# The third expert's second set in one stationary operand: 64 high and 64 low columns

## What is computed

```python
logits = (xt @ router).astype(jnp.float32)
top_logit, top_idx = lax.top_k(logits, TOP_K)          # 2 of 8
gates = jax.nn.softmax(top_logit, axis=-1)
...
yb = _swiglu(xb, w1[e], w3[e], w2[e])                  # silu(x @ w1) * (x @ w3) @ w2, inner width 1408
...
out = jax.ops.segment_sum(y_s * weight_s[:, None].astype(y_s.dtype), token_s, num_segments=T)
```

## Time and profile before

| | us |
|---|---|
| median of 3 runs | 1962.29 |
| lowest, highest | 1961.26, 1963.87 |
| the profiled execution | 1962.09 |
| its span, first to last instruction | 1960.3 |

### The profile page before, as it was taken

One profiled execution on the slowest core, in us unless ns is written; L12 is line 12 of the kernel. 1 busy time (PEld: TensorE's weight loads), 2 busy tenths in 40 slices (PEclk: granted clock), 3 DMA queues, 4 the chain that ended last, 5 costly groups with the idle time before them and its releaser, 6 DMA issues.

```text
span 1960.3 us, 34244 instructions
## 1 busy us (share of the span) xinstructions
PE 1901.8 (97%) x14547; PEld 1749.6 (89%) x14547; DVE 1307.3 (67%) x1851; ACT 941.6 (48%) x1144; POOL 124.2 (6%) x82
## 2 busy tenths in 40 slices
PE   9999999999999999999999999999999999889999
PEld 9889999999988999988788888888888989779988
DVE  7974567645699547666454557888889456866563
ACT  5353344443444433444344346767657443444364
POOL 0000000000000000000101010011200001100034
PEclk9999999999999999999999999999999999999999
DMA  7221345555532123445445467999965323315320
GB/s 306 87 87 57 109 170 204 172 187 179 180 127 87 71 87 135 168 188 174 164 154 180 153 223 276 332 329 333 330 213 184 116 100 124 125 44 173 127 89 23
DMA packets 52679, 321.84 MB, mean 164 GB/s; under 512 B 6320, under 2 KB 9648, under 8 KB 19760
## 3 DMA queue, kind: packets, MB, share of 16 engines
q1 hardware_dynamic: 52096, 317.76, 46.2%
q10 hardware_dynamic: 432, 1.90, 0.3%
HBM read 317.01 MB, written 1.05 MB: 162 GB/s over the span
## 4 chain that ended last, share of the span: by engine, by line
PE 77%; DVE 15%; ACT 4%; issue 3%; DMA 0%; DVEq 0%; ACTq 0%; SPq 0%
PE b L383 76%; DVE s_arena L399 6%; DVE s_ring_lo L501 4%; ACT s_wh L408 2%; PE b L2044 1%; DVE s_arena L402 1%; DVE s_arena L1433 1%; DVE s_arena L2396 1%; ACT s_arena L408 0%; ACT s_arena L405 0%; DVE s_arena L637 0%; DMA s_ring<-experts 0%; DVE s_arena L2320 0%; DVE s_roots L399 0%; DVE s_arena L2317 0%
## 5 line engine op out<-in xcount | busy, mean ns | idle before, releaser
L501 DVE TENSOR_TENSOR s_ring_lo<-s_ring,s_wh 128x2048 fp32r<-128x2048 f32 (+3 forms) x310 | 648.0, 2095 | 315.0 <-ACT s_wh L408 313.9
L408 ACT ACTIVATE s_wh<-s_ring 128x2048 fp32r<-128x2048 f32 (+3 forms) x332 | 574.1, 1732 | 262.8 <-PE b L383 257.1
L383 PE MATMUL b<-s_Hh,s_wh 128*128 128x256 f32 x1832 | 535.3, 292 | 10.0 <-DVE s_arena_r L2923 4.5
L383 PE MATMUL b<-s_Hl,s_wh 128*128 128x256 f32 x1832 | 520.7, 284 | 0.0
L383 PE MATMUL b<-s_Hh,s_ring_lo 128*128 128x256 f32 x1832 | 520.4, 284 | 0.0
L383 PEld LDWEIGHTS b<-s_Hh,s_wh 128*128 128x128 f32 x1832 | 353.5, 193 | 20.9 <-issue 11.0
L383 PEld LDWEIGHTS b<-s_Hl,s_wh 128*128 128x128 f32 x1832 | 353.9, 193 | 0.5
L383 PEld LDWEIGHTS b<-s_Hh,s_ring_lo 128*128 128x128 f32 x1832 | 353.5, 193 | 0.0
L383 PE MATMUL b<-s_wh,s_arena_r 128*128 128x512 f32 (+1 forms) x964 | 305.2, 388 | 3.2 <-DVE s_arena_r L2235 2.6
L383 PE MATMUL b<-s_arena_r,s_wh 128*128 128x256 f32 x1184 | 214.5, 282 | 5.3 <-DVE s_arena L399 2.8
L383 PEld LDWEIGHTS b<-s_wh,s_arena_r 128*128 128x128 f32 x964 | 180.0, 188 | 41.8 <-DVE s_arena_r L2235 3.9
(11 more groups left out here) (193 smaller groups left out, 1962.0 us busy)
## 6 DMA issues: line engine op xcount, KB each, us to landing
s_ring<-fixed SPq DMA_DIRECT2D x158, 1024.0 KB, 4.8
s_ring<-experts SPq DMA_DIRECT2D x96, 1024.0 KB, 5.0
s_ring<-experts SPq DMA_DIRECT2D x48, 768.0 KB, 4.4
s_ring<-fixed SPq DMA_DIRECT2D x24, 256.0 KB, 4.2
s_c<-c SPq DMA_DIRECT2D x1, 1664.0 KB, 17.8
s_ring<-fixed SPq DMA_DIRECT2D x3, 512.0 KB, 6.0
s_arena<-s_arena SPq DMA_DIRECT2D x48, 32.0 KB, 1.9
s_c<-c ACTq DMA_DIRECT2D x1, 1344.0 KB, 6.5
```

Of the source, the lines that this page charges most:

```text
L383: return e.matmul(out, l, r, start=start, stop=True, skip_group_check=True)
L408: return e.activation(out, x, ACT.Copy, scale=scale)
L501: e.tensor_tensor(l_, r_, h_.bitcast(F), SUB).then_inc(*up(engine, z % "lo", i))
```

## The change

The routing now ranks all experts by their count of tokens (key: 8 x count - index), in place of only parting those over 128 from the others. The third turn's second set, (p, s) = (2, 1), is taken to hold 64 slots at most. Its stationary operand of 128 columns holds the high parts of 64 tokens in columns 0..63 and their low parts in 64..127, in `m_H` and likewise in `m_hid`. Two matmuls, with the high and with the low weights, stand where `mm3` had three. The sums of the high parts then stand in rows 0..63 of the bank and those of the low parts in rows 64..127. For gate and up, ACT copies rows 64..127 to `gate_low` or `up_low`, DVE adds rows 0..63, and tanh and multiplies work on 64 rows from there. For down the two row blocks are not added: `m_P` carries the places of the 64 slots twice, so that the scatter adds them. Group 2 is gathered with 192 moving columns in place of 256, and DVE writes its low parts of the packed set beside the high ones.

```diff
@@ routing: order of the experts
-            ts(e, m_ovf, B[5][:, 32:40], 128.0, None, ALU.is_gt).then_inc(*up("V", "ranked"))
-            e.wait_ge(*now("V"))
-            e.tensor_tensor_scan(m_cum, c("ones")[:, 0:8], m_ovf, 0.0, MUL, ADD).then_inc(*up("V"))
...
-            e.tensor_tensor(m_q, m_q, m_d, ADD).then_inc(*up("V"))
+            stt(e, m_key, B[5][:, 32:40], 8.0, c("iota"), MUL, SUB).then_inc(*up("V", "ranked"))
+            e.wait_ge(*now("V"))
+            e.tensor_tensor(m_which, m_key.unsqueeze(1).broadcast_to([128, 8, 8]), m_key.unsqueeze(2).broadcast_to([128, 8, 8]),
+                            ALU.is_gt).then_inc(*up("V"))
+            e.wait_ge(*now("V"))
+            e.tensor_reduce(m_q, m_which, AX.X, ADD).then_inc(*up("V"))
@@ before the expert stage
+        PACKED = {(2, 1)}
+        shared = Arena(22016, 24064)
+        gate_low, gate_sum, up_low, up_sum = (shared(512, p=64) for _ in range(4))
-        PLACES = [128 * sum(SETS[p] for p in ps) for ps in GROUPS]
+        PLACES = [sum(64 if (p, s) in PACKED else 128 for p in ps for s in range(SETS[p])) for ps in GROUPS]
@@ places_dve
+                    for s in range(SETS[p]):
+                        if (p, s) in PACKED:
+                            w_ -= 64
+                            o = offset_of(p, s)
+                            ts(e, m_P[g % 2][:, blk, o + 64:o + 128], c("place")[:, 128 * s:128 * s + 64], m_vp[:, blk, p:p + 1], None,
+                               ALU.is_equal).then_inc(*up("V"))
@@ gather_dve
+            for p, s in PACKED:
+                if GROUP_OF[p] == g:
+                    n_, o = n_ - 64, offset_of(p, s)
+                    for q in range(2):
+                        stt(e, m_H[g % 2][0][:, 2 * jj + q, o + 64:o + 128], b[:, T * q + o:T * q + o + 64], pc("nf1", 2 * jj + q),
+                            m_H[g % 2][0][:, 2 * jj + q, o:o + 64].bitcast(F), MUL, SUB).then_inc(*up("V"))
@@ turn_hidden_pe (n = 64 for the packed unit), turn_hidden_act likewise
-                last = e.transpose(b[:, 128 * j:128 * j + 128], m_vb[t % 2][:, 128 * j:128 * j + 128], ident)
+                last = e.transpose(b[:, 128 * j:128 * j + n], m_vb[t % 2][0:n, 128 * j:128 * j + 128], ident[0:n, 0:n])
@@ turn_hidden_dve
+            if (p, s) in PACKED:
+                part = m_hid[s][0][:, 4 * ch:4 * ch + m, :]
+                e.tensor_tensor(part[:, :, 64:128], b[:, 0:128 * m].rearrange("p (k n) -> p k n", k=m)[:, :, 0:64],
+                                part[:, :, 0:64].bitcast(F), SUB).then_inc(*up("V", "hid lo", p, ch, s))
+                return
@@ expert_up_pe
+                    if (p, s) in PACKED:
+                        both = m_H[g % 2][0][:, 4 * h + kk, o:o + 128]
+                        mm(e, b[:, 0:width], both, wv[0][:, kk, :], h == kk == 0)
+                        last = mm(e, b[:, 0:width], both, wv[1][:, kk, :], False)
+                        continue
@@ expert_down_pe
+                    if (p, s) in PACKED:
+                        mm(e, b[:, :], m_hid[s][0][:, k, :], wv[0][:, k - 4 * j, :], k == 0)
+                        last = mm(e, b[:, :], m_hid[s][0][:, k, :], wv[1][:, k - 4 * j, :], False)
+                        continue
@@ moe_act
-                            for s in range(SETS[p] if k == h == 1 else 0):
+                            for s in range(SETS[p] if h else 0):
                                 t, width = unit[p, ch, s], CHUNKS[ch][1]
+                                if (p, s) in PACKED:
+                                    low, name = (gate_low, "gate low") if k == 1 else (up_low, "up low")
+                                    e.wait_ge(*on(*up_done(p, ch, k, s)))
+                                    if ch:
+                                        e.wait_ge(*on("hidden", t - SETS[p]))
+                                    copy(e, low[:, 0:width], B[t % 2 + (0 if k == 1 else 2)][64:128, 0:width]).then_inc(*up("A", name, t))
+                                if k == 3:
+                                    continue
...
+                                if (p, s) in PACKED:
+                                    e.wait_ge(*on("gate sum", t))
+                                    tanh2(e, m_vb[t % 2][0:64, 0:width], gate_sum[:, 0:width]).then_inc(*up("A", "half tanh", t))
+                                    continue
@@ new, called by moe_dve for the packed unit
+        def packed_dve(e, p, ch, k, s):
+            t, width = unit[p, ch, s], CHUNKS[ch][1]
+            v = m_vb[t % 2][0:64, 0:width]
+            if k == 1:
+                e.wait_ge(*on("gate low", t))
+                e.tensor_tensor(gate_sum[:, 0:width], B[t % 2][0:64, 0:width], gate_low[:, 0:width], ADD).then_inc(*up("V", "gate sum", t))
+                e.wait_ge(*on("half tanh", t))
+                e.wait_ge(*on("gate sum", t))
+                stt(e, v, v, 1.0, gate_sum[:, 0:width], ADD, MUL).then_inc(*up("V", "gate out", t))
+                return
+            e.wait_ge(*on("up low", t))
+            e.tensor_tensor(up_sum[:, 0:width], B[2 + t % 2][0:64, 0:width], up_low[:, 0:width], ADD).then_inc(*up("V"))
...
+            stt(e, v, v, m_gh[0:64, 2 * p + s:2 * p + s + 1], up_sum[:, 0:width], MUL, MUL).then_inc(*up("V", "hidden", t))
```

More of the change, by code:

```diff
@@ L1639, in build @@
         m_idx = m_idx.bitcast(U32)
-        m_ovf, m_cum, m_q, m_d, m_who = (ma(8) for _ in range(5))
+        m_key, m_q, m_who = (ma(8) for _ in range(3))
         m_int = ma(8).bitcast(I32)
@@ L1939, in turns_dve @@
             e.tensor_tensor(m_v, B[5][:, 16:32].rearrange("p (i e) -> p i e", i=2), m_sel, MUL).then_inc(*up("V"))
-            ts(e, m_ovf, B[5][:, 32:40], 128.0, None, ALU.is_gt).then_inc(*up("V", "ranked"))
+            stt(e, m_key, B[5][:, 32:40], 8.0, c("iota"), MUL, SUB).then_inc(*up("V", "ranked"))
             e.wait_ge(*now("V"))
-            e.tensor_tensor_scan(m_cum, c("ones")[:, 0:8], m_ovf, 0.0, MUL, ADD).then_inc(*up("V"))
+            e.tensor_tensor(m_which, m_key.unsqueeze(1).broadcast_to([128, 8, 8]), m_key.unsqueeze(2).broadcast_to([128, 8, 8]),
+                            ALU.is_gt).then_inc(*up("V"))
             e.wait_ge(*now("V"))
-            stt(e, m_q, c("iota"), m_cum[:, 7:8], m_cum, ADD, SUB).then_inc(*up("V"))
-            e.wait_ge(*now("V"))
[L1946 to L1949, removed]
-            e.tensor_tensor(m_q, m_q, m_d, ADD).then_inc(*up("V"))
+            e.tensor_reduce(m_q, m_which, AX.X, ADD).then_inc(*up("V"))
             e.wait_ge(*now("V"))
@@ L2042, in turn_hidden_pe @@
             e.wait_ge(*on("hidden", t))
+            n = 64 if (p, s) in PACKED else 128
             for j in range(CHUNKS[ch][1] // 128):
-                last = e.transpose(b[:, 128 * j:128 * j + 128], m_vb[t % 2][:, 128 * j:128 * j + 128], ident)
+                last = e.transpose(b[:, 128 * j:128 * j + n], m_vb[t % 2][0:n, 128 * j:128 * j + 128], ident[0:n, 0:n])
             last.then_inc(*up("PE", "hidden turned", t))
@@ L2049, in turn_hidden_act @@
             e.wait_ge(*on("hidden turned", unit[p, ch, s]))
-            copy(e, m_hid[s][0][:, 4 * ch:4 * ch + m, :], b[:, 0:128 * m].rearrange("p (k n) -> p k n", k=m)).then_inc(*up("A", "hid hi", p, ch, s))
+            n = 64 if (p, s) in PACKED else 128
+            copy(e, m_hid[s][0][:, 4 * ch:4 * ch + m, 0:n], b[:, 0:128 * m].rearrange("p (k n) -> p k n", k=m)[:, :, 0:n]).then_inc(*up("A", "hid hi", p, ch, s))
         def turn_hidden_dve(e, p, ch, s, b):
@@ L2191, in moe_act @@
             rounds(e, li["exbc", 0])
+        def packed_dve(e, p, ch, k, s):
[11 more added lines that the diff above has]
+            e.wait_ge(*now("V"))
+            e.wait_ge(*on("gate out", t))
+            if ch == 0:
+                e.wait_ge(*on("PT", p, s))
+            stt(e, v, v, m_gh[0:64, 2 * p + s:2 * p + s + 1], up_sum[:, 0:width], MUL, MUL).then_inc(*up("V", "hidden", t))
         def moe_dve(e):
@@ L2220, in moe_dve @@
                                 v = m_vb[t % 2][:, 0:width]
+                                if (p, s) in PACKED:
+                                    packed_dve(e, p, ch, k, s)
+                                    continue
                                 if k == 1:
```

## The result

| | before | after |
|---|---|---|
| median us (lowest to highest), 5 runs each | 1961.9 (1961.26 to 1963.87) | 1944.58 (1942.61 to 1945.42) |
| the profiled execution | 1962.09 | 1944.90 |
| its span | 1960.3 | 1943.1 |

The ratio is 0.9908, with a 95% interval of 0.9898 to 0.9919. The change gains 17.3 us in the medians and 17.2 in the profiled spans; 14.7 were forecast. The direction is right.

What follows compares the result with a forecast made beforehand. TensorE's stream was taken to bound the expert stage, each matmul counting at its pitch. 7.26 + 2.78 + 4.43 + 0.22 + 0.5 - 0.4 - 0.1 = 14.7 us off 1962.1 gave 1947.4 us; range 1944.5 to 1952.5.

Steps and rivals of the forecast that it cites:

- up, less the stall at the turn (2,2,1): Packed set's gate and up: 48 matmuls fewer save 7.26 + 2.78 us; a new stall early in p=3 costs 0.4.
- down, net of the longer wait: Packed set's down: 22 matmuls fewer, three worth nothing as the wait before the second half grows; 4.43 us saved.
- gather: Group 2's gathers: 4 of 8 matmuls with 192 moving columns in place of 256; 0.22 us saved, ends 0 and 0.44.
- small: three turns of 64 rows: The three packed turns use 64 array rows; switching the array's shape costs 0.1 us in all, ends 0 and 0.5.
- routing: Six small DVE steps become three, so all behind them starts 0.5 us sooner, ends 0 and 0.5.
- the pitches: Start-to-start price per matmul: 0.2268 us (up, 512 columns, from H), 0.1735 (384 columns), 0.2333 (down, from the arena).
- pitch still ... 0.233 in the packed units: Sign expected in the profile after: pitch still 0.227, 0.174 and 0.233 us in the packed units.
- (1): Packed chain of ACT and DVE stalls TensorE at three or four places by 1 us each: 1951 us; chance 0.13.
- (2): Weights late: p=3 entered with the ring less full, up to three pieces of lead lost: 1957 us; chance 0.03.
- (3): Dropped matmuls run in the shadow of loads, only 0.11 us won for each of 54: 1956 us; chance 0.02.
- (4): TensorE's shorter pieces all run into the ACT-DVE chain of round and rest (4.3 us): no gain, 1962; chance 0.05.
- (5): ACT and DVE wait for each other in each packed unit, six evacuations overhanging by 3.1 us: slower, 1966; chance 0.05.

Runs made afterwards that it cites:

- a_up3: The changed kernel with a third matmul put back, as a repeat, for each slice of the packed set's gate and up sums; 1952.07 us.
- a_down3: The changed kernel with a third matmul put back, as a repeat, for each slice of the packed set's down sums; 1948.35 us.
- a_p64B: The changed kernel with the tiles behind the small routing tiles moved back up by 64 bytes; 1947.29 us, ratio 0.9927.
- b_route: The kernel before with the new ranking alone, the tiles behind it held in place by a pad of 16 floats; 1962.59 us.
- b_m64B: The kernel before with the tiles behind the small routing tiles moved down by 64 bytes, nothing else; 1957.83 us, ratio 0.9974.
- b_Hstays: The kernel before with everything behind the routing tiles 64 bytes lower except m_H[1], which keeps its place; 1958.46 us.

## Why the prediction was off, point by point

| term, us | forecast | measured | by |
|---|---|---|---|
| up, less the stall at the turn (2,2,1) | 7.26 + 2.78 - 0.4 = 9.64 | 9.77 | a_up3 |
| down, net of the longer wait | 4.43 | 4.39 | a_down3 |
| gather | 0.22 | 0.3 | record lengths, below |
| small: three turns of 64 rows | -0.1 | -0.4 | starts, below |
| all in the stage | 14.19 | 14.07 | a_p64B |
| routing | 0.5 | 0.56 | b_route, after |
| place of the stationary tiles | none | 4.64 | a_p64B, b_m64B |
| up to the routing | none | 0.61 | the cut of the span |
| behind the expert stage | none | -2.68 | the cut of the span |
| sum | 14.7 | 17.2 | |

The gather row is read here (timeline, PE; the earlier trace rows have 1.11 for 256 columns):

```profile
943.62 1.03 PE L383 MATMUL b<-s_arena_r 128*128 128x192 f32 x8
```

0.08 less for one group of eight, four groups, 0.3. The turns of 64 rows were priced too low. The turn of unit (2,1,0) and its neighbours, before and after:

```profile
1096.72 0.39 PE L383 MATMUL b<-s_wh,s_Hl 128*128 128x512 f32 x1
...
1097.31 0.48 PE L383 MATMUL b<-s_wh,s_Hh 128*128 128x512 f32 x1
```

```profile
1088.16 0.39 PE L383 MATMUL b<-s_ring_lo,s_Hh 128*128 128x512 f32 x1
...
1088.87 0.50 PE L383 MATMUL b<-s_wh,s_Hh 128*128 128x512 f32 x1
```

From the last full matmul ahead of the turn to the first behind it are 0.71 us where 0.59 were; 0.09 of the 0.12 lie ahead of the turn's first transpose and 0.03 within it. The second turn costs 0.66 for 0.53, the third, read in a_up3 where it doesn't wait, 0.64 for 0.48: 0.4 in all, inside the forecast's ends of 0 and 0.5. With that the terms read one by one give 9.77 + 4.39 + 0.3 - 0.4 = 14.1, and a_p64B measures 14.07. (The 4.39 was read at the pitch of 0.2271; at 0.2333 the same 19 matmuls are 0.1 more.)

**The step that failed** is in "the pitches": "Down, stationary in the arena, 512 columns: ... 0.2333 each", and with it the use of this number, and of all untouched work, as unchanged. The prediction had two pitches for the same instruction in its own rows, 0.2268 from H and 0.2333 from the arena at the same clock, and priced each without asking what makes them differ. Its sign "pitch still ... 0.233 in the packed units" fails with it: in down it is 0.2271. The term that it put at nothing measured 4.64 us, more than the whole miss of 2.6. The diff held the other half: five scratch tiles become three at the head of an arena in which everything is placed in sequence. "Routing" was costed by its DVE steps alone. The cause is shown by b_m64B (same instructions, 64 bytes, 4.86 us), by a_p64B (the change without the shift lands on 1947.3, where 1947.4 was predicted) and by b_Hstays. What makes the engine slower from such a place stays open.

**The range** was built from the ends of the named costs and from rivals that all cost time. Nothing in it stood for a gain in work that the change doesn't touch. The forecast's own range had 1946.3 as its lower end, from a gain of 15.8; its named ends give only 14.7 + 0.22 + 0.4 + 0.1 = 15.4, so 1946.7. a_p64B's runs (1946.43 to 1948.2) begin just below that.

**Behind the expert stage** the code is the same, yet the stretch takes 541.4 to 544.8 us in the thirteen kernels. The windows between the same two instructions, before and after (columns as in the earlier trace rows):

```profile
1691.27:1746.99 55.72, 43.79 (x394) 36.40 (x395) 43.65 (x111) 26.56 (x62) 7.26 (x10) 0.97 0.08 30
```

```profile
1672.44:1731.31 58.87, 46.94 (x394) 38.57 (x395) 43.79 (x111) 26.56 (x63) 7.26 (x10) 0.91 0.08 28
```

The same 394 matmuls, DVE and ACT busy for the same time, and 3.15 us more with a mean granted clock of 0.91 instead of 0.97, so more of the stretch passed at the lower level (1.2 GHz). The thirteen traces bear this out over the whole stretch. It passed 17.1 to 18.0 us at the lower level in the five that took 541.4 to 541.5 us, 20.5 to 21.4 in the five that took 542.0 to 543.5, and 23.9 in the three that took 544.2 to 544.8. The expert stage passed none of its time there in any of them. This accounts for the 2.68 lost. Whether a kernel draws that clock by when it arrives there, or each execution by chance, one profile for each kernel can't tell; it is why a total from one execution can't be trusted to a microsecond, and why the stage's time was compared instead. The 0.61 us gained ahead of the routing are of this size too: that stretch takes 844.0 to 845.8 us in the thirteen kernels, in no order that follows the changes.

**The rivals.** (1) The packed chain at more places: fell; TensorE's waits in the stage show the forecast two and no other change over 0.3 us, and the up pieces of the packed set keep 0.2284 and 0.174. (2) Late weights: fell, the period is 52.46 as before. (3) Matmuls worth less than their pitch: fell, 48 of them are worth 9.77 with their stall. (4) All pieces running into the chain of round and rest: fell, only the j = 2 piece does. (5) Slower: fell; no evacuation overhangs.

## What to carry to other kernels

A diff that adds or removes a scratch tile moves every tile behind it: list the start of each stationary operand before and after, modulo 256 bytes, as part of the working. Two pitches for the same instruction at the same clock are a question to settle before either is used as a price. And where a wait of TensorE ends on a short step that stands behind a long one in a list worked in order, and that engine idles shortly before, swapping the two can be worth the whole wait (here one moved step took away three waits of 3.7 us together, and the stage got 3.98 us shorter).

## What the runs showed of the hardware that I hadn't expected

With a stationary operand of 128 x 128 in this 4-byte format and 512 moving columns at the full granted clock, the pitch is 0.227 us if the operand starts on a multiple of 256 bytes in its partition, and 0.232 to 0.2335 at 64 or 128 bytes above one, some 0.006 us or 2.7% for each matmul. It was worth 4.6 to 4.9 us of 1960. In turns where the period is set by something else, it was worth next to nothing (0.1 us for two turns). All of this is with a moving operand on a multiple of 256.
